# Expert inputs by indirect transfers through DRAM in place of gathering products

## The reference

```python
def _moe(h, w_router, w_gate, w_up, w_down):
    xf = h.reshape(T, D)                                  # T = 256, D = 1024
    logits = jnp.einsum('td,de->te', xf, w_router)        # 8 experts
    top_logits, top_idx = lax.top_k(logits, TOP_K)        # TOP_K = 2
    gates = jax.nn.softmax(top_logits, axis=-1)
    order = jnp.argsort(top_idx.reshape(-1))
    xs = xf[tok_sorted]                                   # each expert's tokens, one after the other
    hid = silu(ragged_dot(xs, w_gate, sizes)) * ragged_dot(xs, w_up, sizes)   # 1024 -> 3584
    ys = ragged_dot(hid, w_down, sizes)                                       # 3584 -> 1024
    out = zeros.at[tok_sorted].add(ys * gates)
```

## Time and profile before

| | |
|---|---|
| median of the runs | 1959.64 us |
| the profiled execution | 1966.12 us |
| its span | 1964.3 us |
| mean granted TensorE clock | 0.988 |
| TensorE busy | 1900.4 us (97%) |
| VectorE, ScalarE, GpSimd busy | 412.3, 287.0, 40.6 us |
| moved by DMA | 485.83 MB, mean 247 GB/s |
| experts, first gathering product to last product | about 995 to 1947 us |

### The profile page before, as it was taken

One profiled execution on the slowest core, in us unless ns is written; L12 is line 12 of the kernel. 1 busy time (PEld: TensorE's weight loads), 2 busy tenths in 40 slices (PEclk: granted clock), 3 DMA queues, 4 the chain that ended last, 5 costly groups with the idle time before them and its releaser, 6 DMA issues. The chain is left out here.

```text
span 1964.3 us, 29251 instructions
## 1 busy us (share of the span) xinstructions
PE 1900.4 (97%) x13178; PEld 970.0 (49%) x13178; DVE 412.3 (21%) x837; ACT 287.0 (15%) x566; POOL 40.6 (2%) x57
## 2 busy tenths in 40 slices
PE   7999998999999999999989999999999999999996
PEld 4477664457744454558544444444444434444442
DVE  2533233222520000225231010110101111010121
ACT  1210221223210000232211010110101101010110
POOL 0100000001000000001000000000000000000000
PEclk9999999999999999999989999999999999999998
DMA  8742117244224252432549999999999999999991
GB/s 275 236 148 88 44 65 277 99 156 146 71 102 171 86 212 82 174 129 86 184 172 386 384 370 387 366 391 367 379 389 364 389 367 386 386 368 383 382 401 45
DMA packets 221663, 485.83 MB, mean 247 GB/s; under 512 B 14492, under 2 KB 27420, under 8 KB 221405
## 3 DMA queue, kind: packets, MB, share of 16 engines
q1 hardware_dynamic: 213472, 472.02, 65.7%
q10 hardware_dynamic: 6702, 7.03, 1.2%
q0 software_dynamic: 1360, 4.85, 0.6%
HBM read 475.74 MB, written 8.14 MB: 246 GB/s over the span
## 5 line engine op out<-in xcount | busy, mean ns | idle before, releaser
L1288 PE MATMUL bank<-ring,work 128*128 128x512 f32 (+4 forms) x1632 | 676.1, 573 | 18.5 <-ACT work L1502 3.6
L1288 PEld LDWEIGHTS bank<-ring,work 128*128 128x128 f32 x1632 | 307.1, 192 | 359.6 <-issue 326.3
L2755 PE MATMUL bank<-ring,work 128*64 128x512 f32 x1792 | 391.6, 594 | 0.7 <-DVE work L2911 0.7
L2755 PEld LDWEIGHTS bank<-ring,work 128*64 128x64 f32 x1792 | 125.9, 137 | 245.2 <-issue 244.4
L2766 PE MATMUL bank<-ring,work 128*32 128x256 f32 x3584 | 200.0, 380 | 0.0
L2807 PE MATMUL bank<-ring,work 128*64 128x512 f32 x896 | 199.3, 596 | 0.0
L2766 PEld LDWEIGHTS bank<-ring,work 128*32 128x32 f32 x3584 | 113.3, 110 | 97.3 <-issue 26.0
L2807 PEld LDWEIGHTS bank<-ring,work 128*64 128x64 f32 x896 | 61.5, 137 | 120.8 <-issue 120.8
L2920 DVE TENSOR_TENSOR work<-work,bank 64x512 f32<-64x512 f32 x56 | 38.8, 692 | 365.9 <-ACT work L2847 365.9
L2817 PE MATMUL bank<-ring,work 128*32 128x256 f32 x1792 | 103.3, 381 | 0.0
L2847 ACT ACTIVATE work<-bank 64x512 f32<-64x512 f32 x56 | 33.0, 589 | 361.0 <-PE bank L2755 361.0
(11 more groups left out here) (355 smaller groups left out, 1162.1 us busy)
## 6 DMA issues: line engine op xcount, KB each, us to landing
ring<-in_moe_w_gate SPq DMA_DIRECT2D x56, 2048.0 KB, 12.4
ring<-in_moe_w_up SPq DMA_DIRECT2D x56, 2048.0 KB, 10.0
ring<-in_moe_w_down SPq DMA_DIRECT2D x56, 2048.0 KB, 13.5
ring<-in_w_in SPq DMA_DIRECT2D x20, 2048.0 KB, 8.2
ring<-in_w_out SPq DMA_DIRECT2D x6, 2048.0 KB, 9.0
ring<-in_dense_w_gate SPq DMA_DIRECT2D x5, 2048.0 KB, 8.3
ring<-in_dense_w_up SPq DMA_DIRECT2D x5, 2048.0 KB, 7.8
ring<-in_dense_w_down SPq DMA_DIRECT2D x5, 2048.0 KB, 7.8
```

The lines of the kernel that those rows point to most:

```text
L1288: mm = pe.matmul(banks(j)[:, 0:width], x[:, k0 + kt, tt * P:(tt + 1) * P], w[:, kt, c0:c0 + width], start=first and n == 0, stop=last and ...
L2755: mm = pe.matmul(out[half, :], xgT[:, k, 0:64], w[n][:, k, :], start=(k == 0), stop=(k == KD - 1))
```

## The change

1. An internal DRAM tensor `expert_in` of 8 x 96 rows plus 128 spare rows is added. In the last stage of the first block SyncE fills its rows 96 to 767 with zeros by one DRAM to DRAM transfer (2.75 MB, source: one zero row of `shift_rows`, repeated). It stands in SyncE's queue after the squares and bounds (L3311 to L3315) and ahead of the loads of `w_ple_gate` and the next layer's weights (L3316).
2. VectorE works out, for each token and each of its two picks, the row `expert * 96 + rank` of `expert_in`, or a spare row where the rank is over the 96 slots (`dest`, six more small steps).
3. GpSimd then issues four indirect transfers, one after the other, each of which writes 128 rows of 4 KB from `xn` to these rows.
4. For experts 1 to 7 SyncE loads the expert's 96 rows into a new SBUF tile `taken`, ahead of the load with the index 13 of the expert before. For expert 1 SyncE waits there for all four indirect transfers; for the others for the end of the last `gather`, which reads the same tile.
5. `gather(e)` for e of 1 to 7 is 8 transposes of `taken` (96 rows x 128 columns) instead of 16 products. Expert 0 keeps the products. `places` is built for expert 0 and as `gated` for expert 7 only.

```diff
@@ -2636,6 +2636,9 @@
         self.hit, self.row, self.valid = take(NE), take(NT, 2), take(NT, 2)
         self.weight = take(NT, 2)
         self.where = take(NT, 2).bitcast(I32)
+        self.spare = take(1)
+        self.inside, self.goes = take(NT, 2), take(NT, 2)
+        self.dest = take(NT, 2).bitcast(I32)
...
-    place, gated = [take(NT, FIRST) for _ in range(2)], take(NT, FIRST)
+    place, gated = take(NT, FIRST), take(NT, FIRST)
     spreadT = take(SEQ)
+
+
+    taken = take(DM)
 
     fetched = [[take(DM) for _ in range(NT)] for _ in range(2)]
     rows_dram = nc.dram_tensor("expert_rows", ((NE - 1) * FIRST, DM), F32, kind="Internal").ap()
...
         @block.sync
         def _(sp):
             for n in range(SLOTS, NE * LOADS):
                 e, i = n // LOADS, n % LOADS
+                if i == SLOTS + 6 and e + 1 < NE:
+
+                    if e == 0:
+                        sp.wait_ge(rows_spread, 16 * 2 * NT)
+                    else:
+                        sp.wait_ge(gathered, 2 * e + 2)
+                    sp.dma_start(taken[0:FIRST, :], core.expert_in[(e + 1) * FIRST:(e + 2) * FIRST, :])\
+                      .then_inc(taken_in, 16)
                 sp.wait_ge(core.weights_used, used0 + n - SLOTS + 1)
                 sp.dma_start(expert_slot(core, i), expert_weight(a, e, i)).then_inc(core.landed[slot_of(core, i)], 16)
 
...
@@ -2716,17 +2730,24 @@
 
             def gather(e):
                 x = (NC * e) % 2
-                pe.wait_ge(places_ready, e + 1)
+                if e == 0:
+                    pe.wait_ge(places_ready, 1)
+                elif e == NE - 1:
+                    pe.wait_ge(places_ready, 2)
                 if e:
+                    pe.wait_ge(taken_in, 16 * e)
                     pe.wait_ge(hid64, NC * e - 1)
                     pe.wait_ge(hid32, NC * e - 1)
                 for j, bank in enumerate((wide_out[x], narrow_out[x])):
                     for k in range(4):
                         rows = slice((4 * j + k) * P, (4 * j + k + 1) * P)
+                        out = bank[:, k * FIRST:(k + 1) * FIRST]
+                        if e:
+                            mm = pe.transpose(out, taken[0:FIRST, rows], ident[0:FIRST, 0:FIRST])
+                            give_back(mm)
+                            continue
                         for tt in range(NT):
-                            mm = pe.matmul(bank[:, k * FIRST:(k + 1) * FIRST], xn[:, tt, rows], place[e % 2][:, tt, :],
-                                           start=(tt == 0), stop=(tt == NT - 1))
-                            give_back(mm)
+                            mm = pe.matmul(out, xn[:, tt, rows], place[:, tt, :], start=(tt == 0), stop=(tt == NT - 1))
                     if e == NE - 1:
                         mm = pe.transpose(bank[0:FIRST, 384:512], gated[:, j, :], ident)
                     mm.then_inc(gathered, 1)
...
@@ -2876,6 +2897,14 @@
 
         @block.gpsimd
         def _(pool):
+            pool.wait_ge(core.empty_in, 16)
+            pool.wait_ge(dest_ready, 1)
+            for n in range(2):
+                for tt in range(NT):
+                    if n + tt:
+                        pool.wait_ge(rows_spread, 16 * (2 * n + tt))
+                    pool.indirect_dma_start(core.expert_in, bass.IndirectOffsetOnAxis(ap=r.dest[:, tt, n:n + 1], axis=0),
+                                            xn[:, tt, :], None).then_inc(rows_spread, 16)
...
@@ -2895,13 +2924,10 @@
...
-            def places(e):
+            def places(out, factor, e):
                 for tt in range(NT):
-                    last = dve.tensor_scalar(place[e % 2][:, tt, :], slots, r.rank[:, tt, e:e + 1],
-                                             r.chosen[:, tt, e:e + 1], ALU.is_equal, ALU.mult)
-                    if e == NE - 1:
-                        last = dve.tensor_scalar(gated[:, tt, :], slots, r.rank[:, tt, e:e + 1], r.gate[:, tt, e:e + 1],
-                                                 ALU.is_equal, ALU.mult)
+                    last = dve.tensor_scalar(out[:, tt, :], slots, r.rank[:, tt, e:e + 1], factor[:, tt, e:e + 1],
+                                             ALU.is_equal, ALU.mult)
                 last.then_inc(places_ready, 1)
 
...
-            places(0)
+            places(place, r.chosen, 0)
...
                     step(dve.tensor_reduce(r.row[:, tt, n:n + 1], r.hit, AX.X, ALU.add))
-            step(dve.tensor_scalar(r.valid, r.row, FIRST - 0.5, None, ALU.is_lt))
-            step(dve.scalar_tensor_tensor(out=r.valid, in0=r.picks[:, :, 0:2], scalar=NE - 1.5, in1=r.valid, op0=ALU.is_lt, op1=ALU.mult))
+
+            step(dve.tensor_reduce(r.spare, core.before, AX.X, ALU.add))
+            step(dve.tensor_scalar(r.spare, r.spare, float(NE * FIRST), None, ALU.add))
+            step(dve.tensor_scalar(r.inside, r.row, FIRST - 0.5, None, ALU.is_lt))
             step(dve.scalar_tensor_tensor(out=r.row, in0=r.picks[:, :, 0:2], scalar=float(FIRST), in1=r.row, op0=ALU.mult, op1=ALU.add))
+            step(dve.tensor_scalar(r.goes, r.row, r.spare[:, 0:1], None, ALU.subtract))
+            step(dve.tensor_tensor(r.goes, r.goes, r.inside, ALU.mult))
+            step(dve.tensor_scalar(r.goes, r.goes, r.spare[:, 0:1], None, ALU.add))
+            dve.tensor_copy(r.dest, r.goes).then_inc(dest_ready, 1)
+            step(dve.scalar_tensor_tensor(out=r.valid, in0=r.picks[:, :, 0:2], scalar=NE - 1.5, in1=r.inside, op0=ALU.is_lt, op1=ALU.mult))
             step(dve.tensor_tensor(r.row, r.row, r.valid, ALU.mult))
             dve.tensor_copy(r.where, r.row).then_inc(where_ready, 1)
...
-                    if c == 3 and e + 1 < NE:
-                        places(e + 1)
+                    if c == 3 and e + 2 == NE:
+                        places(gated, r.gate, e + 1)
...
@@ -3303,6 +3336,8 @@
             sp.wait_ge(*core.chain_done)
             core.load_weights(sp, everything, most=c_ple[0])
 
+        core.expert_in = nc.dram_tensor("expert_in", (NE * FIRST + P, DM), F32, kind="Internal").ap()
+        core.empty_in = ctx.enter_context(nc.semaphore("empty_in"))
         merge_stage(core, a, f, ya, yb, gates, (c_pa, c_up, c_pb, c_out, c_ple), leads[0])
 
         @core.block.sync
...
@@ -3313,6 +3348,9 @@
             for i in range(2):
                 sp.dma_start(core.out_norms[:, i, :], spread(a["hg_out_norm_2"][i], P)).then_inc(core.later_in, 16)
                 sp.dma_start(core.bounds[:, i, :], spread(a["hg_lower_bounds_2"][i], P)).then_inc(core.later_in, 16)
+            nothing = core.shift_rows[0:1, 0:DM].unsqueeze(0).broadcast_to([NE - 1, FIRST, DM])
+            sp.dma_start(core.expert_in[FIRST:NE * FIRST, :].rearrange("(e s) d -> e s d", s=FIRST), nothing)\
+              .then_inc(core.empty_in, 16)
             core.load_weights(sp, everything, most=core.moe_used)
```

More of the change, by code:

```diff
@@ L2691, in experts_first @@
                "hid64", "hid32", "turned", "hidT_ready", "down64", "down32", "ys_by_vector", "ys_by_scalar",
-               "rows_written", "rows_fetched", "where_ready", "scattered", "added", "vector_steps") as (
+               "rows_written", "rows_fetched", "where_ready", "dest_ready", "rows_spread", "taken_in", "scattered", "added", "vector_steps") as (
             block, places_ready, gathered, xg_ready, gate64, up64, gate32, up32, silu64, silu32,
             hid64, hid32, turned, hidT_ready, down64, down32, ys_by_vector, ys_by_scalar,
-            rows_written, rows_fetched, where_ready, scattered, added, vector_steps):
+            rows_written, rows_fetched, where_ready, dest_ready, rows_spread, taken_in, scattered, added, vector_steps):
         @block.sync
```

## The result

The changed kernel takes 1947.58 us (median of 5 runs, 1944.93 to 1950.06) against 1959.46 us before (5 runs, 1956.74 to 1960.46). The ratio is 0.9943, with a 95% interval of 0.9929 to 0.9958: faster by 11.9 us, where 18.0 were forecast. 1947.58 lies just above the range given, 1939.5 to 1947.5.

A forecast was written before the change was run, and what follows sets the result against it. TensorE, busy 97% of the span, was taken to bound the kernel. Seven gatherings at 2.57 us save 18.0 us, all additions cost nothing: 1959.64 - 18.0 = 1941.6 us, range 1939.5 to 1947.5.

The forecast's parts named there:

- The saving on TensorE: Experts 1 to 7: eight transposes (0.89 to 0.98 us) replace 32 instructions (3.55 us), saving 2.57 us a gathering, 18.0 in all.
- The row of the last expert: Last expert, without a gathering: 1.47 us from turn to turn, against 4.04 with one, taken as the closest spacing possible.
- What was to cost nothing: Work added on VectorE, GpSimd, SyncE, the weight stream and the zero fill: all judged covered, cost taken 0 us.
- the scattering: GpSimd's four indirect transfers: landed by 1035.3, before SyncE issues tile 13 at 1045.94; cost nothing. Being slow: 1972 us, chance 0.05.
- 35.7 us of cover: Delay that the `w_ple_gate` loads behind the zero fill could take: landing at 334.1 and 339.4, used from 369.8 on.
- The 6.8 us: Time of the 2.75 MB zero fill at 407 GB/s, as a plain transfer; outlasting its cover would cost 4 us, chance 0.02.
- rival (1): The clock falls after some 2.0 us of only transposes, seven times: 12 us lost, 1953.5 us, chance 0.04.
- The step that failed: Weight stream in the expert stage: demand rises from 374 to 389 GB/s, a 20 us stretch carries 407, so no cost.
- The term that used up the rest: SyncE's load of `taken` in each expert: 0.39 MB pushes tile 13 back 1.0 us, against 9.4 us of cover; cost nothing.
- its cover once, in expert 0: Tile 13's issue may slip from 1045.94 to 1055.3; the tightest tile has 21 us for a landing of at most 18.1.
- Rival (2): The weight stream becomes the bound, carrying no more than 380 GB/s for long: 9 us lost, 1951 us, chance 0.05.

The follow-up runs named there:

- version with 128 rows: Changed kernel with each expert's rows loaded as 128 rows onto 128 partitions, zero fill as 800 rows split 16 x 50: 1942.14 us; repeated, 1941.04 us.

## Why the prediction was wrong

**The saving on TensorE: right.** Eight transposes held the queue for 0.97 us (1072.40 to 1073.37), where 0.89 to 0.98 was worked out; the wait for VectorE's hidden values set the distance of 1.47 us; the cycles of experts 1 to 4 are 115.3 us as forecast. The version with 128 rows gives the whole 18 us. The row of the last expert, which has no gathering, was the one to trust: it showed what is late next without any estimate.

**What was to cost nothing: right in three cases.** SyncE was not held by the scattering: the load of `taken` for expert 1 goes out at 1030.58, right behind tile 12. The four indirect transfers start at 1001.65, 1005.46, 1009.56 and 1017.83 and land after 3.5 to 8.0 us, about as the fetches of the earlier trace rows. The fill delayed the loads of `w_ple_gate`, from a landing of 10.1 and 14.9 us to 25.2, and this stayed under its 35.7 us of cover: they are there at 344.1 and 349.4 and first used near 363.8. The rule of the Trainium skill (DMA: Bandwidth & Descriptors, Rules for kernel authors) on a leading broadcast gave an estimate of 15.5 us for the fill, and the trace agrees with it: the engines' share of 0.45 is that of 7 of 16, and the packets start over 18.4 us. The 6.8 us that the prediction took for a plain transfer were too low for another reason as well, since the fill split by 16 was no faster. The clock stayed at 1.00 through the 2 us of transposes, so rival (1) didn't come.

**The step that failed** is the weight stream: "A stretch of 20 us carries 407 GB/s, so there is room." The 407 was read in a stretch that holds only down tiles; what a stream of all tiles can carry was taken from its fastest part. Two thirds of an expert's bytes are gate and up tiles with rows of 2 KB, and these move at 387 GB/s. With the right rates an expert's tiles take 29.4 MB at 0.387 MB/us and 14.7 at 0.409, 111.9 us; with the output rows and `taken`, 0.39 MB each, it is 113.9 us: still under the 115.3 of TensorE, by 1.4 us and not by the 5 us that 407 GB/s had promised.

**The term that used up the rest** is the load of `taken`: "It pushes tile 13 back by 0.39 MB at 380 GB/s, 1.0 us." It was priced by its bytes. It costs 2.0 us more, since it goes onto 96 partitions: 115.9 us. Measured, from landing to landing of tile 13: 117.1. Of the missing 1.2 us, 0.9 belong to the tiles and the output rows (112.9 by these rates, 113.8 measured without `taken`) and 0.3 to the narrow load; the 0.9 are not explained. By either number the demand is above what TensorE gives time for, so the backlog grows with each expert. The prediction asked whether a tile's landing fits its cover once, in expert 0; it had to ask what happens to the landing from one expert to the next. Tile 13 lands at 1053.7 in expert 0 and is used from 1061.4, 7.7 us later; at 117.1 - 115.3 = 1.8 us an expert this is gone in expert 5, where TensorE first waits.

Rival (2) had the mechanism, a stream that can't go faster than some 380 GB/s, and 1951 us for it; its reason was another one (bytes, not a slow load), and it got 0.05. In the changed kernel the stream moved 44.8 MB in 117.1 us, 383 GB/s. The row that spoke for it was in sight: a DMA share of 1.02 at 380 GB/s, that is engines with little time left at a rate below 407; where they never idle the share is 1.03 to 1.05.

How a narrow load comes to disturb the tile beside it was not tried.
## What to carry to other kernels

Where an edit shortens the engine that bounds a stage with a saturated stream beside it, compare the stream's time for a whole period, kind of transfer by kind, with the new period, and follow the landing times from period to period: cover that is large once is used up by a small excess that repeats. Small loads in such a stream should have the shape of its large ones: here 128 rows, of which 32 are thrown away, are 5 to 8 us better than the 96 that are needed. And a wait that the profile puts down to an engine long done is another's: look for the transfer that lands at that instant.

## What was not expected of the hardware

- A load onto 96, 64 or 32 partitions in the midst of loads onto 128 lowers the rate of all of them for some microseconds: 386 to 389 GB/s become 270 to 342 over 4 us, and 292 over 8 us where the queue is full. A second one right behind it lengthened the cycle by a further 3.2 us (116.9 to 120.1).
- A DRAM to DRAM fill from one repeated row moved 174 GB/s split by 7, at a share of 0.45, and 198 GB/s split by 16, at 1.04: more engines, hardly more speed.
- Tiles of 2 MB with rows of 2 KB move at 387 GB/s, with rows of 4 KB at 409, with the DMA engines fully busy in both (shares of 1.05 and 1.03).
- SyncE's issue of a load, 0.37 us otherwise, takes 4 to 7 us where the queue is full (5.29 us for `taken` at 1615.09, 6.90 at 1030.58, long before TensorE waits). It is a sign of a full queue, not of time lost: in the version with 128 rows, in which TensorE never waits for a tile, the issue of `taken` takes 3.6 to 5.4 us in every expert.
